# A hybrid decoder layer in fp32 on one core: a fourth seven-product unit in some blocks, another order on VectorE and a fourth rounded slot

## What is computed

```
x += 1/2 * SwiGLU_1(norm(x))        # FFN, D_FF = 5504 = 43 tiles of 128
x += concat(MLA(norm(x)), HGRN2(norm(x))) @ W_out   # "mixer": one projection W_in feeds both
x += CrossAttention(norm(x), norm(mem))
x += 1/2 * SwiGLU_2(norm(x))
SwiGLU(h) = (silu(h @ w_gate) * (h @ w_up)) @ w_down
```

## Time and profile before

| | |
|---|---|
| median of 3 runs | 1881.78 us (1881.56 to 1881.98) |
| span of the profiled execution | 1880.3 us |
| TensorE busy | 1874.0 us, 8808 matmuls |
| VectorE busy | 1606.9 us |
| ScalarE busy | 1096.4 us |
| read from HBM | 358.95 MB, 192 GB/s over the span |

### The profile page before, as it was taken

One profiled execution on the slowest core, in us unless ns is written; L12 is line 12 of the kernel. 1 busy time (PEld: TensorE's weight loads), 2 busy tenths in 40 slices (PEclk: granted clock), 3 DMA queues, 4 the chain that ended last, 5 costly groups with the idle time before them and its releaser, 6 DMA issues.

```text
span 1880.3 us, 23355 instructions
## 1 busy us (share of the span) xinstructions
PE 1874.0 (100%) x8808; PEld 1570.5 (84%) x8808; DVE 1606.9 (85%) x2077; ACT 1096.4 (58%) x1496; POOL 95.2 (5%) x98
## 2 busy tenths in 40 slices
PE   9999999999999999999999999999999999999999
PEld 8888888888889888988888888888888888888987
DVE  6999999989999868787677764789999999999986
ACT  7665555555656547556476655656555565555553
POOL 0000000000000002312260000000000000000000
PEclk9999999999999999999999999999999999999999
DMA  9666655666556664456443654456555566665654
GB/s 338 224 197 200 195 197 194 226 202 201 180 184 211 219 230 155 137 165 227 144 152 108 220 184 136 157 190 195 197 192 194 199 209 214 201 199 183 194 193 171
DMA packets 176753, 362.58 MB, mean 193 GB/s; under 512 B 8576, under 2 KB 19840, under 8 KB 176000
## 3 DMA queue, kind: packets, MB, share of 16 engines
q1 hardware_dynamic: 176208, 360.89, 57.6%
q10 hardware_dynamic: 432, 0.19, 0.0%
HBM read 358.95 MB, written 2.10 MB: 192 GB/s over the span
## 4 chain that ended last, share of the span: by engine, by line
PE 88%; DVE 9%; issue 2%; ACT 1%; DMA 0%; DVEq 0%; SPq 0%; ACTq 0%
PE acc L2090 16%; PE acc L2092 16%; PE acc L2091 16%; PE acc L2079 8%; PE acc L2081 8%; PE acc L2080 8%; DVE w_lo L1376 5%; PE small L2090 2%; PE small L2092 2%; PE small L2091 2%; PE small L2291 2%; PE tr L2038 2%; PE tr L2090 1%; PE tr L2092 1%; PE tr L2091 1%
## 5 line engine op out<-in xcount | busy, mean ns | idle before, releaser
L1376 DVE TENSOR_TENSOR w_lo<-w_raw,w_hi 128x1024 fp32r<-128x1024 f32 (+3 forms) x784 | 760.2, 1025 | 52.8 <-ACT w_hi L765 40.5
L765 ACT ACTIVATE w_hi<-w_raw 128x1024 fp32r<-128x1024 f32 (+4 forms) x566 | 497.6, 916 | 132.3 <-PE acc L2092 105.9
L2090 PE MATMUL acc<-w_hi,hT_hi 128*128 128x512 f32 (+1 forms) x960 | 371.0, 386 | 0.1
L2092 PE MATMUL acc<-w_lo,hT_hi 128*128 128x512 f32 (+1 forms) x960 | 368.9, 384 | 0.0
L2091 PE MATMUL acc<-w_hi,hT_lo 128*128 128x512 f32 (+1 forms) x960 | 368.6, 384 | 0.0
L870 ACT ACTIVATE w_hi<-w_raw 128x1024 fp32r<-128x1024 f32 (+1 forms) x192 | 198.7, 1045 | 125.7 <-DVE w_raw L1364 76.9
L1305 DVE TENSOR_TENSOR w_lo<-w_raw,w_hi 128x1024 fp32r<-128x1024 f32 (+1 forms) x166 | 197.1, 1229 | 24.9 <-ACT w_hi L765 23.3
L863 ACT ACTIVATE w_hi<-w_raw 128x512 fp32r<-128x512 f32 (+1 forms) x192 | 155.7, 831 | 92.3 <-PE acc L2092 89.0
L2090 PEld LDWEIGHTS acc<-w_hi,hT_hi 128*128 128x128 f32 x960 | 180.2, 188 | 34.9 <-DVE w_lo L1376 0.6
L2092 PEld LDWEIGHTS acc<-w_lo,hT_hi 128*128 128x128 f32 x960 | 180.2, 188 | 34.2
L2091 PEld LDWEIGHTS acc<-w_hi,hT_lo 128*128 128x128 f32 x960 | 180.3, 188 | 33.3
(11 more groups left out here) (344 smaller groups left out, 2628.8 us busy)
## 6 DMA issues: line engine op xcount, KB each, us to landing
w_raw<-in_ffn_w_down SPq DMA_DIRECT2D x56, 768.0 KB, 4.7
w_raw<-in_ffn_w_down SPq DMA_DIRECT2D x40, 1024.0 KB, 5.3
w_raw<-in_ffn_w_gate SPq DMA_DIRECT2D x58, 512.0 KB, 3.9
w_raw<-in_ffn_w_gate SPq DMA_DIRECT2D x38, 768.0 KB, 4.4
w_raw<-in_ffn_w_up SPq DMA_DIRECT2D x38, 768.0 KB, 4.5
w_raw<-in_w_in SPq DMA_DIRECT2D x28, 1024.0 KB, 5.1
w_raw<-in_ffn_w_up SPq DMA_DIRECT2D x54, 512.0 KB, 4.8
w_raw<-in_ffn_w_up SPq DMA_DIRECT2D x26, 1024.0 KB, 5.9
```

The costliest lines, as they stand in the source:

```text
L765: nc.scalar.activation(piece(w_hi, c % SPLIT, k0, k1, width), piece(raw, c % RAW, k0, k1, width), ACT.Copy).then_inc(hi_done, 1)
L1376: v.tensor_tensor(piece(w_lo, c % RAW, k0, k1, width), piece(raw, c % RAW, k0, k1, width), piece(w_hi, c % SPLIT, k0, k1, width).bitcast(F ...
L2090: mm(dst, lhs_hi, wh, start=first, stop=False)
L2092: return mm(dst, lhs_hi, wl, start=False, stop=last)
```

## The change

- SPLIT goes from 3 to 4 (one more slot of `w_hi`), and the scratch of dynamic DMAs shrinks to make room.
- A duo gets a list `later` for its seconds beside `plains`. In each FFN the up duos (half, block) = (0, 2), (0, 4), (1, 1), (1, 3) get four units with firsts of 2, 2, 2, 2 tiles and seconds of 4, 4. The down duos of the second half get four units and plains of 3, 3, 3, 2. H_SUMS and A_SUMS, the numbers of activation sums kept, go to 4 and (5, 4).
- A plain slot of two tiles is rounded and subtracted in one operation of 1024 columns, not two of 512.
- On VectorE `combine` falls into `first_sums` (made 0 and 1) and `other_sums` (made 2, raw part 0's w_lo, made 3); work of the plain before stands between them, and `turn_round_lo(m, 0)` stands directly behind `other_sums`, ahead of raw part 1's w_lo (`other_raw`). `take_first` moves behind all seconds.
- p5 stays in its accumulator, so `take_parts` has three adds, and TensorE does side 1's first plain for token tile 0 whole before it waits for `parts_taken`.
- On ScalarE the two Silu move behind the seconds and the next duo's `hi_raw`; `flat_x` makes four flat copies.
- The mixer's own pair of blocks (PAIR) gets seconds of 4, 2, 2 tiles and the same order.

```diff
-SPLIT = 3
+SPLIT = 4
+        UP3 = ("upupup", [0, 2, 4], [(6, 4), (10, 3), (13, 3)], [(6, 4), (10, 3), (13, 3)])
+        UP4 = ("upupupup", [0, 2, 4, 6], [(8, 2), (10, 2), (12, 2), (14, 2)], [(8, 4), (12, 4)])
+        FOUR = [(0, 2), (0, 4), (1, 1), (1, 3)]
+        DOWN = [("upupupupup", [0, 2, 4, 6, 8], 2 * [(10, 3), (13, 3), (16, 3), (19, 3), (22, 2)]),
+                ("upupupup", [0, 2, 4, 6], 2 * [(8, 3), (11, 3), (14, 3), (17, 2)])]
...
-                    DUOS.append(Duo(f, True, h, b, min(4, tiles - 4 * b) * P, "upupup", [0, 2, 4], [(6, 4), (10, 3), (13, 3)]))
+                    DUOS.append(Duo(f, True, h, b, min(4, tiles - 4 * b) * P, *(UP4 if (h, b) in FOUR else UP3)))
...
             def hi(c, rep, tiles, width, part=None):
 
                 c += rep
+                if tiles == 2:
+                    act.wait_ge(loaded[c % RAW], landed(c))
+                    act.wait_ge(slot_used, freed(c, 1))
+                    nc.scalar.activation(piece(w_hi, c % SPLIT, 0, 2, width), piece(raw, c % RAW, 0, 2, width), ACT.Copy).then_inc(hi_done, 2)
+                    return
...
                         hi_raw(e.raws[0], e.width)
+                        if d.up:
+                            for t in range(TT):
+                                act.wait_ge(ev("first_taken"), TT * m + t + 1)
+                                nc.scalar.activation(gate[:, t, 0:w], gate[:, t, 0:w], ACT.Silu,
+                                                     scale=cols(rsq, NAMES[f], t, 1)).then_inc(ev("gated"), 1)
...
+            def other_sums(c, n, width, made_sem="combined"):
+
+                b, made = weight_tiles(c, width), weight_tiles(c + 1, width)
                 dve.wait_ge(ev(made_sem), 2 * n + 1)
                 done(v.tensor_tensor(made[:, 2, :], b[:, 3, :], made[:, 0, :], ALU.subtract))
+                split(c, 0, *RAW_PARTS[0], width).then_inc(lo_done, 1)
                 done.wait()
                 v.tensor_tensor(made[:, 3, :], b[:, 2, :], made[:, 2, :], ALU.subtract).then_inc(ev(made_sem), 1)
...
-                done(v.tensor_tensor(gate[:, 1, 0:w], p7, nat[:, 0, 0:w], ALU.add))
-                done(v.tensor_tensor(nat[:, 0, 0:w], p5, nat[:, 0, 0:w], ALU.add))
-                done.wait()
-                v.tensor_tensor(nat[:, 1, 0:w], p5, gate[:, 1, 0:w], ALU.add).then_inc(ev("parts_taken"), 1)
+                done(v.tensor_tensor(nat[:, 1, 0:w], p7, nat[:, 0, 0:w], ALU.add))
+                v.tensor_tensor(nat[:, 0, 0:w], p5, nat[:, 0, 0:w], ALU.add).then_inc(ev("parts_taken"), 1)
...
                         if kind == "u" and n:
-                            combine(d.raws[n], u0 + n, w)
-                            lo_parts(d.raws[n], RAW_PARTS, w, u0 + n)
+                            first_sums(d.raws[n], w)
+                            if d.order[:2 * n].endswith("p"):
+                                plain_lo(d.firsts[n - 1], d.plains[n - 1][1], w)
+                                if n == 1 and m > m0 and DUOS[m - 1].up:
+                                    multiply_up(m - 1)
+                                if n == 2 and turns_in(d):
+                                    turn_round_lo(m, 1)
+                            other_sums(d.raws[n], u0 + n, w)
                             if n == 1 and turns_in(d):
                                 turn_round_lo(m, 0)
-                            lo_parts(d.raws[n] + 1, MADE_PARTS, w)
+                            other_raw(d.raws[n], u0 + n, w)
+                            made_lo(d.raws[n] + 1, w)
...
+                if side == 1 and n == 0:
+                    for kk in range(tiles):
+                        half(kk)
+                        tile(kk, 0)
+                    pe.wait_ge(ev("parts_taken"), m + 1)
+                    for kk in range(tiles):
+                        ins = tile(kk, 1)
```

More of the change, by code:

```diff
@@ L94 @@
     plains: list
+    later: list
     raws: list = field(default_factory=list)
@@ L115, in place @@
                 c += 1
-        for n in range(len(self.plains)):
+        for n in range(len(self.later)):
             self.seconds.append(c)
@@ L154, in layer @@
     SCALE, X_SCALE = float(QK) ** -0.5, float(P) ** -0.5
+    H_SUMS, A_SUMS = 4, (5, 4)
     ctx = ExitStack()
@@ L541, in load_duos @@
                             load_constants(m)
-                    for n, (k, tiles) in enumerate(d.plains):
+                    for n, (k, tiles) in enumerate(d.later):
                         load_plain(d.seconds[n], 1, k, tiles)
@@ L611, in load_pair @@
                     load(PAIR.firsts[n], 0, rows_of(a["w_in"][0], k, tiles, sides[0]), tiles, NW)
-                for n, (k, tiles) in enumerate(PAIR.plains):
+                for n, (k, tiles) in enumerate(PAIR.later):
                     load(PAIR.seconds[n], 0, rows_of(a["w_in"][0], k, tiles, sides[1]), tiles, NW)
@@ L839, in flat_x @@
             def flat_x():
-                for n in range(H_SUMS):
+                for n in range(4):
                     act.wait_ge(tr_ready[n % 2], groups["x_o"] + n // 2 + 1)
@@ L1687, in pair @@
                 done.wait()
[L1688 to L1691, removed]
-                lo_parts(PAIR.seconds[1], PLAIN_PARTS[PAIR.plains[1][1]], NW)
+                done(v.tensor_tensor(nat[:, 1, :], p7, nat[:, 0, :], ALU.add))
+                v.tensor_tensor(nat[:, 0, :], p5, nat[:, 0, :], ALU.add).then_inc(ev("mix_parts_taken"), 1)
+                plain_lo(PAIR.seconds[1], PAIR.later[1][1], NW)
                 dve.wait_ge(slot_used, 2 * (PAIR.firsts[-1] + 1))
@@ L1701, in pair @@
                 dve.sem_inc(ev("forgets_summed"), 1)
-                for n in (2, 3):
-                    lo_parts(PAIR.seconds[n], PLAIN_PARTS[PAIR.plains[n][1]], NW)
+                plain_lo(PAIR.seconds[2], PAIR.later[2][1], NW)
                 forget(1)
@@ L2161, in plain, with tile, half @@
                 d = DUOS[m]
-                c, (k0, tiles), w = (d.firsts, d.seconds)[side][n], d.plains[n], d.width
+                c, (k0, tiles), w = (d.firsts, d.seconds)[side][n], (d.plains, d.later)[side][n], d.width
                 hi_, lo_ = (hT_hi, hT_lo) if d.up else (actT_hi, actT_lo)
-                last, mid = n == len(d.plains) - 1, (tiles + 1) // 2
-                for kk in range(tiles):
+                last, mid = n == len((d.plains, d.later)[side]) - 1, (tiles + 1) // 2
+                def tile(kk, t):
+                    at_ = slice(t * P, (t + 1) * P)
+                    return product(acc[:, GB[d.f] if side == 0 else 1 - GB[d.f], t, 0:w], hi_[:, k0 + kk, at_], lo_[:, k0 + kk, at_], c, kk, w,
+                                   False, last and kk == tiles - 1, goes_on=side == 1 and t == 1)
+                def half(kk):
                     if kk in (0, mid):
@@ L2183, in last_plain @@
                 d = DUOS[m]
-                c, (k0, tiles) = d.seconds[-1], d.plains[-1]
+                c, (k0, tiles) = d.seconds[-1], d.later[-1]
                 pe.wait_ge(lo_done, 2 * c + 2)
@@ L2210, in duos @@
                             plain(m, 0, n, (lambda: turn_round(m, 0)) if n == 0 and turns else None)
-                    for n in range(len(d.plains)):
-                        if m == LAST[2] and n == len(d.plains) - 1:
+                    for n in range(len(d.later)):
+                        if m == LAST[2] and n == len(d.later) - 1:
                             last_plain(m)
```

169 lines of the change are left out of this document (95 added, 74 removed).

## The result

The changed kernel takes 1914.12 us (median of 4 runs, 1913.51 to 1914.34) against 1881.86 for the one before: 1.0171 times as long, 95% interval 1.0157 to 1.0185. Forecast was 1912. The profiled execution spans 1912.5 us. One of the 11 runs of `three_late` in experiment 6 was a slow one of 3011.53 us, the others took 1880.82 to 1881.99, and its ratio is of those alone.

A forecast was written before the change was run, and what follows sets the result against it. TensorE bound the kernel, with VectorE near it. Net of saved matmuls, stalls of 7.6 and 7.7 us in an FFN's halves gave +30.6 over two FFNs: 1880.3 to 1910.9 profiled, plus 1.5 for the runs' median, 1912; range 1890 to 1922.

The forecast's parts named there:

- 36 matmuls, 8.2 us: Four up duos and two late down duos per FFN save one product each, all on TensorE's path: 8.2 us.
- The load fits but the place doesn't: VectorE needs 82.5 us a pair against 84.2, but waits for the turned block ahead of a deadline in unit 1.
- The chain of 2.34 and 2.79 us, hence a wait of 1.73 and 2.18: From unit 1's last sum to the turned block's w_lo: 2.34 us, 2.79 with flat copy; VectorE idles 1.73 or 2.18.
- The deadline rule: Stall is VectorE's step end + 0.24 less TensorE's own time; 1.93 us at a 4-unit duo's raw part 1.
- Dependent operations start on time in the new order: In VectorE's unit sums, 0.11 and 0.12 of lateness go as other work stands between: 0.23 us a unit.
- The down duo: First down duo, w_lo wanted at 9.99 and done at 10.93: stall 1.18 against 0.32 before, +0.86 us.
- The narrow block: Second half's block 4, of 384 columns: raw part 1 wanted at 8.8, done at 10.43, +1.87 us.
- First pair, 0 to +1 and taken as 0: First pairs get a fourth token sum, ScalarE two more flat copies: 0 to +1 us each, taken as 0.
- covered and faster: Rival: the turn's wait falls where TensorE has enough ahead, so only the matmuls count: 1873 us; chance 0.12.
- by load alone: Rival: deadlines give way and VectorE's summed work decides the duo lengths: 1897 us; chance 0.16.
- as late as before: Rival: dependent operations on VectorE keep their late starts, 4.1 us more an FFN: 1920 us; chance 0.03.
- stalls that just eat the matmuls: Rival: 4-unit duos lose 0.7 us, not 2.6, cancelling the saving: 1880 to 1883 us; chance 0.05.

The follow-up runs named there:

- three_late: Changed kernel without its added units, the turned block's w_lo behind raw part 1's, old numbers of activation sums; 1881.3 us, 0.9997 of the kernel before.
- experiment 6: The run of `three_late`: changed kernel without added units, the turned block's w_lo behind raw part 1's, old numbers of activation sums; 1881.3 us.
- best: `turn_mid` with up-duo fourth units only in first half block 1 and second half block 0, ScalarE's squares behind the first pair's last rounding; 1884.4 us.
- Experiments 1, 4 and 5: `turn_late`, `turn_mid`, and the changed kernel with ScalarE's copies of the turned block ahead of rounding made part 1 of unit 1 (1891.95 us).
- experiment 3: The run of `before_turn_early`: kernel before, the turned block's w_lo moved directly behind unit 1's weight sums, ahead of its raw w_lo; 1920.5 us, 1.0205.
- down_units: `turn_mid` with three units in all up duos, a fourth only in late down duos, three activation sums for up units; 1880.4 us, 0.9992.
- three_units: Changed kernel without its added units: three units in every up duo and late down duo, all else kept; 1897.8 us, 1.0083 of the kernel before.
- turn_late: Changed kernel with the turned block's w_lo moved behind raw part 1's w_lo of unit 1; 1891.9 us, 1.0052 of the kernel before.
- turn_mid: Changed kernel with the turned block's w_lo moved between the two w_lo of unit 1's made tiles; 1883.1 us, 1.0007 of the kernel before.
- best_oldpair: `best` with ScalarE's old order in the first pair; 1883.1 us, 1.0004 of the kernel before.
- before_turn_early: Kernel before, with the turned block's w_lo moved directly behind unit 1's weight sums, ahead of its raw w_lo; 1920.5 us, 1.0205.

## Why the prediction was right, point by point

- *36 matmuls, 8.2 us*: held. They are gone (8808 to 8772). Where a fourth unit brings no stall, block 0 of the second half in `best`, three of them are worth 0.70 us.
- *The load fits but the place doesn't*: held, and is the point of the case. Experiments 1, 4 and 5 change no more than where one operation stands on VectorE or ScalarE, and the time moves over 31 us; experiment 3 does so in the kernel before, and it moves by 39.
- *The chain of 2.34 and 2.79 us, hence a wait of 1.73 and 2.18*: measured 1.61 and 2.10. From the start of the last sum to the start of the turned block's w_lo are 2.29 us in block 4, not 2.34, and 2.78 with the copy (101.33 to 104.11), not 2.79.
- *The deadline rule*: the first stall of block 4 was 1.84 against 1.93, and four duo lengths in a row came out within 0.05 us.
- *Dependent operations start on time in the new order*: the operations from 188.84 to 190.04 are 0.60 and 0.60 apart, where the old ones were 0.73 and 0.61 apart. The Trainium skill (VectorE: DVE Perf Modes, "The DRAIN you can't avoid") has a semaphore after each of eight copies cost nothing extra. In this case's traces a wait for the operation directly ahead goes with 0.11 to 0.12 us (1.25 against 1.14, 0.73 against 0.61); whether the semaphore or the dependence costs it, no run separates. But `three_late` shows that these savings buy no time, since TensorE was at its pace; they only make room.
- *The down duo*: +0.86 was wrong. Its first stall is 1.08 us as forecast (1.18), but the kernel before had three more small ones, of about 0.3 each, in the early down duos (I counted one place), and the new order removes them. The stretch from the early down duo's T0 to block 1's got 0.3 shorter in FFN 1 and 0.2 in FFN 2, not 0.9 longer.
- *The narrow block*: 34.0 us in FFN 1 and 34.4 in FFN 2 against 34.6, so +1.87 should have been about 1.3 and 1.6.
- *First pair, 0 to +1 and taken as 0*: mis-sized. FFN 1's first transposes come at 59.89, not 57.78: +2.1. TensorE stalls 0.6 and 1.2 us there for w_lo. Its cause is settled in part. From the first matmul of block 1 to those transposes are 8.99 us in the changed kernel and 7.65 before, 8.46 and 8.57 with three sets of activation sums for up units (`three_late`, `down_units`), 9.03 with four and other places of the line (`three_units`, `turn_late`, `turn_mid`, within 0.02). So the fourth set goes with about 0.5 us; 0.8 comes with something else of the change, and 0.8 lies ahead of that matmul (50.90, before 50.13), both left open. ScalarE's squares of x are not the cause: with them moved the stall of 1.1 us is still there, and others come on top (60.03 in `best`, 58.17 in `best_oldpair`).
- *Between the FFNs*: from the first late down duo's transposes in FFN 1 to the first ones in FFN 2 the change adds 1.3 us. My sum had 0.1 for the late down duos and nothing for the mixer and the second first pair.
- *Second half, block 1*: 0.9 over the forecast in each FFN. In the profiled execution this is the clock, see below; nothing in my steps had it.

Errors up (first pair 2.1, between the FFNs 1.2, clock 0.9 in each FFN: about 5) and down (early down duos 1.1 in each FFN, narrow blocks 0.8 together: about 3) cancel in large part, so that 1912 came so near to 1914 is partly luck; the duo lengths are the better test of the mechanism.

The rivals: "covered and faster" falls with the wait rows; "by load alone" (1897) falls with the duo lengths, 44.8 and 43.9, or 88.7 for a pair where it had 86.9; "as late as before" (1920) falls with the steps of 0.60; and 1914 is far above the 1880 to 1883 of stalls that just eat the matmuls.

## What to carry to other kernels

When two engines run level, sum each engine's work, but then walk through the feeding engine's list in order (here VectorE's), from the last point where it must wait for the other, and set every hand-over against its deadline: work behind that point can't be brought forward past it. An operation that waits for a third engine belongs behind whatever the bound engine needs next, with as much other work ahead of it as its chain is long. And before buying cheaper arithmetic on the bound engine with work on another, look where in the period that work falls, not only whether it fits.

## What the runs showed of the hardware

TensorE's granted clock fell after some of its stalls. In the second half's block 1 of the changed kernel TensorE falls 2.2 us behind its pace waiting for w_lo (the row below shows 2.07 of it as idle). Right behind it the mean clock of a stretch of 4.2 us is 0.59, which comes to some 3.4 us at half speed (1.2 GHz) and the rest at full speed (2.4 GHz). Busy times by stretches (TensorE, weight loads, VectorE, ScalarE, GpSimd, clock, DMA share, GB/s), and the matmuls there:

```profile
445.00:450.30 5.30, 3.23 (x16) 2.42 (x15) 3.20 (x5) 2.98 (x4) 0.00 (x0) 1.00 0.83 281
450.30:454.50 4.20, 4.20 (x15) 3.39 (x14) 4.20 (x5) 1.60 (x4) 0.00 (x0) 0.59 0.29 64
454.50:460.00 5.50, 5.50 (x26) 4.57 (x25) 5.46 (x7) 4.94 (x7) 0.00 (x0) 1.00 0.39 148
```

```profile
449.74 0.50 PE L2130 MATMUL acc<-w_hi,hT_hi 128*128 128x512 f32 x1 [2.07 <-DVE w_lo L1384]
450.07 0.39 PE L2131 MATMUL acc<-w_hi,hT_lo 128*128 128x512 f32 x1
...
450.54 0.62 PE L2130 MATMUL acc<-w_hi,hS_hi 128*128 128x512 f32 x1
450.95 0.63 PE L2131 MATMUL acc<-w_hi,hS_lo 128*128 128x512 f32 x1
451.38 0.63 PE L2132 MATMUL acc<-w_lo,hS_hi 128*128 128x512 f32 x1
```

Matmuls start 0.41 to 0.43 apart at 450.54 and behind, not 0.23, and the duo is 0.9 us longer than its twin. It happens at the same block in FFN 2 (the stretch 1652 to 1660 has a clock of 0.79), once in `before_turn_early` (at 153.5, after a shorter stall, 1.5 us of idle time), and nowhere in `turn_late` or `turn_mid`. But the same stall in block 2 of the first half, 2.2 us in each FFN, left the clock alone, so a stall of this length does not always bring it. What decides was not tried.

Over whole runs its price isn't shown. The four runs of the changed kernel had mean clocks of 0.998, 0.998, 1.000 and 0.999 and took 1914.34, 1914.19, 1914.05 and 1913.51 us: the run without a fall is 0.3 us below the profiled one, where two falls at 0.9 would be 1.8.
